# Gate blocks of the input projection in fewer and longer groups between the steps of the attention

## The reference, cut to what matters

```python
(a_q, a_k, a_v, i_q, ...) = jnp.split(xn @ w_in, points, axis=-1)
o_a = softmax attention over the keys a top-k picks   # mixer A
o_b = stick-breaking attention:                       # mixer B
      la = log_sigmoid(-z); after = reverse cumsum(la) - la
      a = exp(log_sigmoid(z) + after); o = a @ v
o_c = softmax attention with a forget bias            # mixer C
branch = einsum('btnw,nwd->btnd', o, w_branch)
gate = sigmoid((xn @ w_gate).reshape(B, T, 3, D_MODEL))
out = einsum('btnd,btnd->btd', gate, branch) @ w_out
```

## Time and profile before

| what | us |
|---|---|
| median of 3 runs | 2195.29 (2191.95 to 2202.59) |
| the profiled execution | 2195.33 |
| its span, first to last instruction | 2193.5 |
| PE busy | 2148.7 (98%) |
| DVE busy | 1342.6 (61%) |
| ACT busy | 955.0 (44%) |
| POOL busy | 196.0 (9%) |
| mean granted TensorE clock | 0.995 of full |

### The profile page before, as it was taken

The page is one execution under the profiler, slowest core; times in us unless marked ns, Lnnn a source line. Parts: engine busy times, 40 slices in busy tenths (PEclk is TensorE's granted clock), DMA queues, the critical chain, the costliest instruction groups (busy, mean ns, idle before and its releaser), DMA issues.

```text
span 2193.5 us, 40057 instructions
## 1 busy us (share of the span) xinstructions
PE 2148.7 (98%) x16226; PEld 2023.5 (92%) x16226; DVE 1342.6 (61%) x2486; ACT 955.0 (44%) x1543; POOL 196.0 (9%) x144
## 2 busy tenths in 40 slices
PE   7999999999999999999999999999999999999997
PEld 7798999897899999999998889888979999999997
DVE  6558636765566773576365686377656477636753
ACT  3346414634634662344332572156255266524432
POOL 0000000000022110011310100000000311100122
PEclk9999999999999999999999999999999999999998
DMA  5231133121122223222232212221211222232223
GB/s 193 59 108 40 58 97 111 40 78 39 49 78 77 86 86 87 87 85 87 96 104 68 92 39 87 84 95 49 71 40 55 84 80 80 88 91 86 86 87 103
DMA packets 51795, 176.10 MB, mean 80 GB/s; under 512 B 6032, under 2 KB 8672, under 8 KB 51664
## 3 DMA queue, kind: packets, MB, share of 16 engines
q1 hardware_dynamic: 44496, 158.81, 23.4%
q0 software_dynamic: 2848, 10.54, 1.2%
q10 hardware_dynamic: 4320, 4.87, 0.7%
HBM read 161.30 MB, written 12.90 MB: 79 GB/s over the span
## 4 chain that ended last, share of the span: by engine, by line
PE 96%; DVE 3%; ACT 1%; DMA 0%; issue 0%; SPq 0%; DVEq 0%; ACTq 0%
PE d L1230 61%; PE d L1273 14%; PE ab L1306 4%; PE ab L1527 2%; PE d L1570 2%; PE d L1579 2%; PE d L1306 1%; PE d L1444 1%; PE ab L1352 1%; PE ab L1230 1%; PE ab L1557 1%; PE ab L1519 1%; PE ab L1520 1%; DVE ol L813 1%; PE ab L1257 0%; PE d L1398 0%
## 5 line engine op out<-in xcount | busy, mean ns | idle before, releaser
L410 ACT ACTIVATE wh<-raw 128x512 fp32r<-128x512 f32 x580 | 365.7, 631 | 839.6 <-PE d L1230 697.0
L710 DVE TENSOR_TENSOR wl<-raw,wh 128x512 fp32r<-128x512 f32 x580 | 402.8, 696 | 410.0 <-ACT wh L410 400.6
L1230 PE MATMUL d<-xh,wh 128*128 128x288 f32 x2400 | 513.9, 295 | 17.7 <-DMA cf<-in_const 14.5
L1230 PE MATMUL d<-xl,wh 128*128 128x288 f32 x2400 | 510.4, 293 | 0.0
L1230 PE MATMUL d<-xh,wl 128*128 128x288 f32 x2400 | 510.4, 293 | 0.0
L1230 PEld LDWEIGHTS d<-xh,wh 128*128 128x128 f32 x2400 | 383.1, 188 | 21.2 <-DMA cf<-in_const 14.5
L1230 PEld LDWEIGHTS d<-xh,wl 128*128 128x128 f32 x2400 | 382.6, 188 | 0.0
L1230 PEld LDWEIGHTS d<-xl,wh 128*128 128x128 f32 x2400 | 382.4, 188 | 0.0
L1273 PE MATMUL d<-xh,wh 128*128 128x288 f32 x768 | 174.8, 309 | 0.0
L1273 PE MATMUL d<-xh,wl 128*128 128x288 f32 x768 | 164.9, 296 | 0.0
L1273 PE MATMUL d<-xl,wh 128*128 128x288 f32 x768 | 164.8, 296 | 0.0
(11 more groups left out here) (309 smaller groups left out, 3197.9 us busy)
## 6 DMA issues: line engine op xcount, KB each, us to landing
raw<-in_w SPq DMA_DIRECT2D x290, 512.0 KB, 3.5
out_o_k<-k POOLq DMA_DIRECT2D x4, 1152.0 KB, 7.2
out_o_v<-v POOLq DMA_DIRECT2D x4, 1024.0 KB, 8.7
x<-in_xT SPq DMA_DIRECT2D x8, 288.0 KB, 6.4
out_y<-z SPq DMA_DIRECT2D x8, 288.0 KB, 2.3
k<-in_bc_k_past ACTq DMA_DIRECT2D x4, 512.0 KB, 4.7
v<-in_bc_v_past ACTq DMA_DIRECT2D x4, 512.0 KB, 5.6
cf<-in_const SPq DMA_DIRECT2D x1, 896.0 KB, 8.1
```

The costliest lines, as they stand in the source:

```text
L410: act.activation(wh[:, c % SPLIT_SLOTS, :], raw[v_ % 2][:, (c % 2) * 512:(c % 2) * 512 + 512], ACT.Copy).then_inc(high_done, 1)
L710: dve.tensor_tensor(wl[:, c % SPLIT_SLOTS, :], raw[(c // 2) % 2][:, (c % 2) * 512:(c % 2) * 512 + 512], wh[:, c % SPLIT_SLOTS, :].bitcast( ...
L1230: ins = pe.matmul(outs[half], w_, r_[:, kk, HALF * half:HALF * half + HALF], start=first and n == 0, stop=last and n == len(kks) - 1)
```

## The change

Only the order of PE's instructions in the pairs is changed; the same matmuls are issued. DVE, ACT, POOL and SP have the same program as before. In a stick-breaking pair the groups of gate blocks, before 4, 4, 3, 5 blocks (8, 3, 5 in the first pair), become 8, 3, 5, and each stands elsewhere. In a softmax pair they were 4, 4, 2, 2, 4 and become 8, 2, 3, 3.

```diff
@@ stick-breaking pair
-                            if p == 0:
-                                pe.wait_ge(dfree[1 - gate_bank(m)], freed(l, D_G[m] + 1))
-                                logits_x(p)
-                                gate_blocks(l, m, 0, range(0, 8))
-                                pe.wait_ge(v_ready, l * 2 + m + 1)
-                            else:
+                            if p:
                                 pe.wait_ge(atts, t3 - 2)
                                 logits_y(p)
...
                                 values(p - 1)
-                                gate_blocks(l, m, 2 * p, range(0, 4))
+                            gate_blocks(l, m, 2 * p, range(0, 8))
+                            if p == 0:
+                                pe.wait_ge(dfree[1 - gate_bank(m)], freed(l, D_G[m] + 1))
+                                pe.wait_ge(v_ready, l * 2 + m + 1)
+                            else:
                                 pe.wait_ge(o_ready, l * 3 * PAIRS + p)
-                                logits_x(p)
-                                gate_blocks(l, m, 2 * p, range(4, 8))
+                            logits_x(p)
                             pe.wait_ge(sp_los_pool, b + 1)
                             pe.wait_ge(sp_los, 2 * b + 1)
                             sums_y()
                             sums_z()
+                            gate_blocks(l, m, 2 * p + 1, range(0, 3))
                             pe.wait_ge(sp_hxs, b + 1)
                             later_x()
-                            gate_blocks(l, m, 2 * p + 1, range(0, 3))
+                            gate_blocks(l, m, 2 * p + 1, range(3, 8))
                             pe.wait_ge(sp_los, 2 * b + 2)
                             sums_x()
-                            gate_blocks(l, m, 2 * p + 1, range(3, 8))
@@ softmax pair
-                            if p:
-                                gate_blocks(l, m, 2 * p, range(0, 4))
+                            gate_blocks(l, m, 2 * p, range(0 if p else 4, 8))
...
                             turn(0)
                             pe.wait_ge(exps, t4 + 1)
                             score_tiles(p, ((1, 0, 0),))
-                            gate_blocks(l, m, 2 * p, range(4, 8))
+                            gate_blocks(l, m, 2 * p + 1, range(0, 2))
                             pe.wait_ge(scaled, t4 + 2)
                             pe.wait_ge(pts, t4 + 1)
                             turn(1)
                             pe.wait_ge(exps, t4 + 2)
                             apart(pe)
                             scores_samples(p)
-                            gate_blocks(l, m, 2 * p + 1, range(0, 2))
+                            gate_blocks(l, m, 2 * p + 1, range(2, 5))
                             pe.wait_ge(scaled, t4 + 3)
                             pe.wait_ge(pts, t4 + 2)
                             turn(2)
-                            gate_blocks(l, m, 2 * p + 1, range(2, 4))
                             pe.wait_ge(scaled, t4 + 4)
                             turn(3)
                             if p < PAIRS - 1:
                                 scores_wide(p + 1)
                                 scores_next(p + 1)
-                            gate_blocks(l, m, 2 * p + 1, range(4, 8))
+                            gate_blocks(l, m, 2 * p + 1, range(5, 8))
```

## The result

The changed kernel takes 2317.61 us (median of 4 runs, 2311.01 to 2323.92), the kernel before 2195.36 beside it (4 runs, 2191.95 to 2202.59): ratio 1.0552, 95% interval 1.0504 to 1.06. The forecast was 2308 us, the range 2268 to 2338. The profiled execution of the changed kernel took 2311.5 us, its span 2309.7; the sum of the prediction, 2307.8, was made for such an execution.

What follows compares the result with a forecast made beforehand. PE, busy 98% of the span, was taken to bound the kernel. Terms of B 10.2, C 38.4 and A 29.9 us made 78.5, with the clock's 34 112.5; 2195.3 + 112.5 gave 2308 us, range 2268 to 2338.

Steps and rivals of the forecast that it cites:

- The softmax waits: In the softmax pairs (C, A), tile 2p+1 waits for DVE's `gate_take(2p)`: 4.65 us in C, 4.8 in A.
- The last pair's 0.5 us ahead of `values`: Last softmax pair of a branch: PE waits 0.5 us for ACT's `turn_step(3)` before `values`.
- The switches between groups: One gate-block group fewer per pair, 24 in all, saves switches between blocks and attention steps: -2.2 us.
- The two old waits: Waits in the first pairs of B and A vanish: -1.31 and -2.46 us per layer, -4.5 us for the clock.
- The clock: PE's clock falls at each of 16 softmax pairs, costing 2.1 us each, 34 us; bounds 0 and 3.4 each.
- B: Stick-breaking pairs: a loop through PE and DVE plus waits in the last pair cost 5.1 us per layer.
- The loop's two waits: Stick-breaking pairs: the next even tile's first block waits for DVE's take, 1.5 or 1.6 us, twice per layer.
- DVE's split of the output: Last stick-breaking pair: DVE's split behind `values` comes another 0.6 us later, between 0 and 2.4.
- Rival 1: The waits come but the clock hardly falls: 2274 us, chance 0.15.
- rival 2: The clock stays low longer after each wait, 3.4 us, and falls at B's 1.6 us waits: 2337 us, chance 0.08.
- rivals 3 and 4: 3: bank wait is off the path, 2181 us, chance 0.02; 4: softmax stalls below 0.7 us, 2205 us, 0.03.

Runs made afterwards that it cites:

- e1: Changed kernel with DVE's `gate_take(2p)` moved ahead of `low_parts` in the softmax pairs; PE's new order stays: 2204.17 us, ratio 1.0039.
- e5: New PE order in the softmax pairs only, stick-breaking pairs as in the kernel before: 2304.45 us, ratio 1.0497.
- e8: Kernel before, with gate blocks moved only into its two old waits, and `gate_take(0)` early in A's first pair: 2185.56 us, ratio 0.9946.
- e2: New PE order in the stick-breaking pairs only, softmax pairs as in the kernel before: 2207.85 us, ratio 1.0041.
- e7: Kernel before, PE's old order, with `gate_take(2p)` (softmax) and `gate_take(2p+1)` (stick-breaking) moved earlier on DVE: 2211.59 us, ratio 1.0076.
- e3: Changed kernel with 44 unread bf16 matmuls put into each softmax wait ahead of tile 2p+1: 2276.87 us, ratio 1.0347.
- e4: Changed kernel with `gate_take(2p)` of the softmax pairs moved between the low part and the maximum, a shorter wait: 2256.62 us, ratio 1.0272.
- e6: Changed kernel with `gate_take(2p)` ahead of the low part (softmax) and `gate_take(2p+1)` between the top-k rounds (stick-breaking): 2199.37 us, ratio 1.0004.

## Why the prediction was right, and where its terms were off

**The softmax waits** (forecast 4.65 and 4.8 us, 16 times) are the mechanism, as e1 shows by taking them away and e5 by having them alone. They measure 4.46 in C and 4.57 in A. The instant of the take was read to 0.01 us; PE came 0.2 later than 1.92 us behind `turn(0)`. The last pair's 0.5 us ahead of `values` was 0.34 to 0.37 (the row of L1577).

**The switches between groups** (-2.2 us) gave nothing, and this step failed. It counted one group fewer in each of 24 pairs; the first pairs of B and A have as many as before, so it is 20. And with the waits gone, a pair of C with one group fewer takes 24.06 us (e1) for 24.03. The first kind of matmul did fall as forecast, 309 to 306 ns in e1's page, but it is the mean of a row's duration and not a distance between starts; by the starts in the two timelines the 16 blocks take 13.20 us for 13.27, as forecast, but `turn(2)` and `turn(3)`, now back to back, take 0.86 us for 0.77, and so the saving is given back. Why they take longer was not tried. So the change had no gain but that of the two old waits.

**The two old waits** went, with their low clock, as forecast (-1.31 and -2.46 per layer, -4.5 for the clock): e8 measures 8.2 us in A for a forecast 9.4, and 2.8 in B for 2.6. The 4.5 for the clock was luck in part: the prediction took the falls behind both 2.46 us waits as a property of the kernel, but of six such waits in the profiles of the kernel before, e2 and e7 only three show one. Forecast and result are both compared with the one execution that had two.

**The clock** (16 falls at 2.1 us) came at all 16 pairs, 13 times in the profiled execution for some 6.8 us at the low level and three times for 3.4 (a 17th stood in B). The difference of the C and A stages between the changed kernel and e3 is 10.74 + 9.50 + 8.23 + 8.34 = 36.8 us, 2.3 a fall; the low time is some 99 us there, so 0.37 of it was lost, less than the 0.45 read from eight transpositions, since part of the low time lies in the wait. (The medians differ by 40.7, but they hold the two lengths of the feed-forward part told below.) The Trainium skill ("TensorE: Matmul & The Clock Gate", HAM oscillation) puts such a loss at half of the low time; by that it would be 50 us here, an estimate from the 99 us, and e3 shows 37. The term was sized right through two errors that cancel: falls longer than the 4.7 us each that 2.1 at 0.45 stands for, and a lower share lost.

**B** (5.1 us per layer) measured 5.61 in layer 1 and 7.86 in layer 0. The loop's two waits were 1.59 for 1.5 or 1.6, `values` 1.11 for 1.3. Missed by name was `branch_first`: 0.89 us for the bank that `gate_take(7)` frees, where the prediction had 0.6 for DVE's split of the output. In layer 0 there are also a first wait of 1.98 instead of 1.59 and a fall of the clock behind it (that period is 29.97 us, the next 28.46, so 1.5); the other 0.4 us lie ahead of the pairs, where the code is the same (114.57 us for 114.18).

**Total.** Forecast +112.5, the profiled execution +116.2, the medians +122.3. The stages account for the 116. The rest lies between executions: the four runs are 2311.5, 2323.73, 2323.92 and 2311.01. Of two profiles with a longer time at the same code, e1's has 429.77 us between the norm's products (L1242) ahead of and behind the feed-forward part of layer 0, where the kernel before and the changed one have 419.05; e2's has some 10 us more in layer 1. In e1 it is no wait of PE and no fall of the clock: the rows of the products there are 296 ns for 292. What sets it stays open. Rival 1 (no clock loss, 2274) is what e3 made on purpose, 2276.87; rival 2 had the longer falls right, but they cost 2.3 us each and not 3.4, and B's 1.59 us waits drew none; rivals 3 and 4 fell with the first row of the waits.

## What to carry over

Before work is moved on the engine that bounds a kernel, ask for each moved group which buffer it opens and where, on the other engine, the instruction stands that frees it: the old order was late by design, and the new one met a take 4.5 us ahead of its time, 16 times. A move that needs a free buffer earlier has to come with the move that frees it (e1), and the one without the other costs either way round (the change, e7). Where the bounding engine is 98% busy, as here, what was to be had lay in its waits: filling those by themselves gave 0.5% (e8), and regrouping what is already dense gave nothing. And a fall of the clock in one profile is not yet a property of the kernel: look for it in a second one before its price goes into a sum.

## What was not expected of the hardware

- An idle stretch of PE can cost more than its length, and the same stretch does not always do. Counted over the ten profiles: waits of 1.31 and 1.59 us inside the pairs drew no fall of the clock; of five waits of 1.98 or 1.99 us in B two did (the changed kernel and e4, not e1, e2, e3); of 16 of 1.96 or 2.07 us in e4 twelve did, each of 3.4 us at 1.2 GHz; of six of 2.46 us three did (both before, one of two in e7, none in e2), with waits of 1.14 and 0.82 us shortly ahead of each; of 32 of 4.46 or 4.57 us all did (the changed kernel and e5), 28 of them for 6.8 us. One fall each in e1 and e6 stands behind a wait of only 0.52 us (the product L1306, layer 1; L1305 in e6), so the length of the last wait does not decide it alone.
- Matmuls that nobody reads, in the place of a wait, make the kernel faster: 37 us by the profiled executions in e3, for 704 extra ones.
- In the changed kernel 0.37 of the time at the low clock was lost, since part of it passes while PE still waits; behind A's old wait it was 3.03 of 6.8 us and 1.41 of 3.4 (before against e2).
